# A two-layer streaming encoder on one core: last scaling on ScalarE, one transpose earlier, two orders changed where the down units open

## The reference

```python
for layer in range(DEPTH):                       # two layers: mixer A, then mixer B
    x = x + 0.5 * swiglu_ffn(rms_norm(x, ffn1_norm[layer]), ...)
    x = x + mixer(rms_norm(x, mix_norm[layer]))
    x = x + 0.5 * swiglu_ffn(rms_norm(x, ffn2_norm[layer]), ...)
return rms_norm(x, final_norm)

def swiglu_ffn(x, w_gate_up, w_down):
    g, u = split(x @ w_gate_up)
    return (silu(g) * u) @ w_down
```

## Time and profile before

| | us |
|---|---|
| three runs: median, lowest, highest | 1786.98, 1783.23, 1788.59 |
| the profiled execution: time | 1787.7 |
| its span | 1785.8 |
| PE busy | 1723.8 (97% of the span) |
| DVE busy | 1411.4 (79%) |
| ACT busy | 1009.8 (57%) |
| POOL busy | 434.9 (24%) |

### The profile page before, as it was taken

The page is one execution under the profiler, slowest core; times in us unless marked ns, Lnnn a source line. Parts: engine busy times, 40 slices in busy tenths (PEclk is TensorE's granted clock), DMA queues, the critical chain, the costliest instruction groups (busy, mean ns, idle before and its releaser), DMA issues. The chain is left out here.

```text
span 1785.8 us, 35301 instructions
## 1 busy us (share of the span) xinstructions
PE 1723.8 (97%) x12929; PEld 1612.4 (90%) x12929; DVE 1411.4 (79%) x2769; ACT 1009.8 (57%) x2008; POOL 434.9 (24%) x495
## 2 busy tenths in 40 slices
PE   8999999999999999999999999999999999999996
PEld 7999999977899999998999999987867889999995
DVE  6887887667778878867788788767897778878788
ACT  6564665446665655555665565543565556565552
POOL 2333333011023333330233333200000043333310
PEclk8999999999999999999999999999999999999998
DMA  6999899443449998994699989834112389998961
GB/s 189 203 202 212 193 200 237 100 116 90 135 104 201 199 218 196 202 220 128 132 205 201 212 200 203 195 100 120 28 41 60 124 182 200 208 214 194 209 160 48
DMA packets 170377, 293.80 MB, mean 165 GB/s; under 512 B 22689, under 2 KB 56670, under 8 KB 170206
## 3 DMA queue, kind: packets, MB, share of 16 engines
q0 software_dynamic: 66816, 121.66, 39.8%
q1 hardware_dynamic: 101824, 168.13, 31.0%
q10 hardware_dynamic: 1566, 1.74, 0.3%
HBM read 163.29 MB, written 2.10 MB: 93 GB/s over the span
## 5 line engine op out<-in xcount | busy, mean ns | idle before, releaser
L2004 PE MATMUL bank<-h_all,w_all 128*128 128x256 f32 x2352 | 671.9, 286 | 23.7 <-ACT work L1131 11.3
L2005 PE MATMUL bank<-h_all,w_all 128*128 128x256 f32 x2352 | 665.9, 283 | 0.0
L2006 PE MATMUL bank<-h_all,w_all 128*128 128x256 f32 x2352 | 665.8, 283 | 0.0
L829 POOL DMA_DIRECT2D work<-r_all x348 | 306.6, 1021 | 964.1 <-DVE w_all L1323 589.6
L2004 PEld LDWEIGHTS bank<-h_all,w_all 128*128 128x128 f32 x2352 | 451.3, 192 | 35.1 <-DVE w_all L1323 20.1
L2005 PEld LDWEIGHTS bank<-h_all,w_all 128*128 128x128 f32 x2352 | 451.6, 192 | 0.0
L2006 PEld LDWEIGHTS bank<-h_all,w_all 128*128 128x128 f32 x2352 | 451.6, 192 | 0.0
L1323 DVE TENSOR_TENSOR w_all<-work,w_all 128x512 fp32r<-128x512 f32 x352 | 234.0, 687 | 106.7 <-ACT w_all L947 106.1
L1323 DVE TENSOR_TENSOR w_all<-r_all,w_all 128x512 fp32r<-128x512 f32 (+1 forms) x356 | 300.0, 864 | 2.5 <-ACT w_all L947 0.4
L947 ACT ACTIVATE w_all<-r_all 128x512 fp32r<-128x512 f32 (+1 forms) x356 | 266.5, 768 | 58.2 <-PE bank L2006 56.8
L947 ACT ACTIVATE w_all<-work 128x512 fp32r<-128x512 f32 x352 | 209.4, 622 | 101.9 <-PE bank L2006 55.3
(11 more groups left out here) (226 smaller groups left out, 2673.3 us busy)
## 6 DMA issues: line engine op xcount, KB each, us to landing
work<-r_all POOLq DMA_DIRECT2D x348, 256.0 KB, 4.7
r_all<-ffn_gu SPq DMA_DIRECT2D x88, 512.0 KB, 5.0
r_all<-r_all POOLq DMA_DIRECT2D x116, 256.0 KB, 6.5
r_all<-ffn_gu SPq DMA_DIRECT2D x88, 256.0 KB, 6.0
work<-ffn_gu SPq DMA_DIRECT2D x88, 256.0 KB, 5.1
r_all<-ffn_d SPq DMA_DIRECT2D x32, 512.0 KB, 5.0
x_f<-ffn_e SPq DMA_DIRECT2D x24, 384.0 KB, 5.3
work<-ffn_d SPq DMA_DIRECT2D x32, 256.0 KB, 4.3
```

The costliest lines, as they stand in the source:

```text
L829: pool.dma_start(chain[g % CHAIN], plain[(u + 2) % 3][:, part * S:(part + 1) * S], accum_op=ALU.add).then_inc(chain_sum[g % CHAIN], 16)
L2004: t.matmul(o, wh, xh, start=c == 0 and not on, stop=False, skip_group_check=on)
L2005: t.matmul(o, wh, xl, start=False, stop=False, skip_group_check=on)
L2006: last = t.matmul(o, wl, xh, start=False, stop=c == PAIRED - 1, skip_group_check=on)
```

## The change

There are four edits.

1. At the end, the scaling of both halves moves from DVE to ACT (`scaled_out`). DVE makes one more small instruction a tile, the whole factor in `st[:, 5]`. ACT squares tile i and then scales tile i-1; the last tile is scaled behind all squares. DVE's order in a tile is now: both sums, the first gain, the mean, the second gain, the factor.
2. One of the twelve squares behind the units moves into unit 28, behind fill FC.
3. In units 9 and 21 (`mixed_late`) the split of the last pair moves: on ACT behind the copy `u_3`, on DVE behind the opening unit's first addition to x.
4. At the openings P6(u) stands ahead of P3(u-1), as everywhere else.

```diff
+def mixed_late(u):
+    return u in COMBINED and opening(u + 1)
...
 def product_order():
...
-        late = [(3, u - 1), (6, u)] if opening(u) else [(6, u), (3, u - 1)]
-        out += [(1, u), (2, u), (4, u - 1)] + late + [(5, u), (7, u)]
+        out += [(1, u), (2, u), (4, u - 1), (6, u), (3, u - 1), (5, u), (7, u)]
...
 # scalar block, ffn
-                    if q is not None:
+                    if q is not None and not mixed_late(u):
                         high_mixed(y_mix, combine_count(f, q, True), q % PAIRED)
                     if gate:
                         act.wait_ge(prod_done, product_count(f, 7, u))
                         act.wait_ge(e_5, at)
                         a.activation(u_3, b[:, 0:HN], ACT.Copy).then_inc(e_7, 1)
+                    if mixed_late(u):
+                        high_mixed(y_mix, combine_count(f, q, True), q % PAIRED)
...
 # scalar block, the end
+            def scaled_out(i):
+                act.wait_ge(tok_rms, i + 1)
+                act.wait_ge(tok_o, 2 * i + 2)
+                for half in range(2):
+                    o = o_stage[:, (2 * i + half) * S:(2 * i + half + 1) * S]
+                    a.activation(o, o, ACT.Copy, scale=st[:, 5, i:i + 1]).then_inc(tok_out, 1)
             for i in range(TT):
                 for half in range(2):
                     act.wait_ge(tok_x, 2 * i + half + 1)
                     a.activation(xg[:, half, :], x_final(i, half), ACT.Square, scale=D ** -0.5,
                                  accum_out=sm[:, half, 0, i:i + 1]).then_inc(tok_sq, 1)
+                if i > 0:
+                    scaled_out(i - 1)
+            scaled_out(TT - 1)
...
 # vector block, ffn
                     if opening(u):
                         dve.wait_ge(prod_done, product_count(f, 1, u))
                         x_added(UNITS[u][2], 0, b).then_inc(e_1, 1)
+                    if mixed_late(u - 1):
+                        q = COMBINED[u - 1]
+                        low_mixed(y_mix, combine_count(f, q, True), q % PAIRED)
                     low_fill(f, FU, u + 1)
...
                     low_fill(f, FC, u)
                     if q is not None:
                         mix(q % 2, k, 2)
+                    if f == FFNS - 1 and u == NU - 2:
+                        x_turned(range(4, 5))
...
-                    if q is not None:
+                    if q is not None and not mixed_late(u):
                         low_mixed(y_mix, k, q % PAIRED)
...
 # vector block, the end
-            x_turned(range(2 * (NU - 3 - DOWN_END[1]), TT * TT))
+            x_turned(range(5, TT * TT))
...
+            for i in range(TT):
+                token_sum(i, 0)
+                token_sum(i, 1)
+                token_gain(i, 0)
+                token_mean(i)
+                token_gain(i, 1)
+                token_factor(i)
...
 # in token_factor, in place of the two scalings
+                v.tensor_scalar(st[:, 5, one], st[:, 4, one], st[:, 1, one], None, ALU.mult).then_inc(tok_rms, 1)
```

More of the change, by code:

```diff
@@ L582, in build @@
         tok_out = sem("tok_out")
+        tok_o = sem("tok_o")
+        tok_rms = sem("tok_rms")
         block = ctx.enter_context(nc.Block())
@@ L1910, in _, with token_sum, token_gain, token_mean @@
             dve.wait_ge(xt_done, TT * TT)
-            for i in range(TT):
-                one = slice(i, i + 1)
[L1913 to L1921, removed]
+            def token_sum(i, half):
+                at = 2 * i + half
+                x_t = x_final(i, half)
+                dve.wait_ge(tok_full, at + 1)
+                v.scalar_tensor_tensor(x_t, TOK[at][:, :], -0.5, x_t, ALU.mult, ALU.add).then_inc(tok_x, 1)
+            def token_gain(i, half):
+                at = 2 * i + half
+                dve.wait_ge(tok_x, at + 1)
+                v.tensor_tensor(o_stage[:, at * S:(at + 1) * S], x_final(i, half), sq[:, half, :], ALU.mult
+                                ).then_inc(tok_o, 1)
+            def token_mean(i):
+                one = slice(i, i + 1)
                 dve.wait_ge(tok_sq, 2 * i + 2)
@@ L1924, in _, with token_factor @@
                                 ).then_inc(tok_mean, 1)
+            def token_factor(i):
+                one = slice(i, i + 1)
                 dve.wait_ge(pow_done, count["stat"] + i + 1)
@@ L1928, in _ @@
                 tok_done(v.tensor_scalar(st[:, 4, one], st[:, 2, one], -0.5, 1.5, ALU.mult, ALU.add))
-                for half in range(2):
-                    v.tensor_scalar(o[half], o[half], st[:, 4, one], st[:, 1, one], ALU.mult, ALU.mult
-                                    ).then_inc(tok_out, 1)
+                v.tensor_scalar(st[:, 5, one], st[:, 4, one], st[:, 1, one], None, ALU.mult).then_inc(tok_rms, 1)
[6 more added lines that the diff above has]
+                token_factor(i)
         @block.tensor
@@ L2056, in ffn @@
                     product(f, 4, u - 1)
[L2057 to L2062, removed]
+                    product(f, 6, u)
+                    product(f, 3, u - 1)
                     product(f, 5, u)
```

## The result

The changed kernel is slower: 1793.0 us median of 19 runs (1784.7 to 1797.68) against 1784.5 (1780.31 to 1788.59, 19 runs) for the kernel before. The ratio is 1.0042, interval 1.0029 to 1.0054, so 7.5 us; the two medians differ by 8.5. The forecast was 1787.9, with a range up to 1791.5: +0.9 us on 1786.98, the median of the first three runs of the kernel before, which is 2.5 above that of all 19. The profiled execution of the changed kernel took 1794.84 us with a span of 1793.0, 7.2 us more than the span before.

A forecast was written before the change was run, and what follows sets the result against it. PE was taken to bound the kernel, with time to win only at its waits and the end after it. Openings +3.7, square 0, token tiles -2.8 make +0.9 us on the 1786.98 median: 1787.9, range 1780.5 to 1791.5.

The forecast's parts named there:

- Behind P7, PE and DVE are late by the same 0.46: After each opening's wait: both engines stay 0.46 us late, so nothing beyond that delay is lost or gained.
- the price of edits 3 and 4: At the eight openings: moved splits and new product order cost +3.7 us, bounds -2.8 and +9.1.
- the slower one: At openings, FB's split starts only where it started before, losing the whole 1.14 us slot: 1793.3 us, chance 0.10.
- Edits 3 and 4, DVE's list: At each opening DVE waits for FB's high part, so its list gets 0.46 us later and P7 waits 2.0 us.
- P6 ahead of P3: At openings the new order gives nothing, since P6 had long ended when DVE came to its addition.
- Edit 2: Square moved into unit 28: DVE's 1.26 us delay is passed around, so 0; bound -1.26.
- the sign that the prediction gave for it: At the end, the squares should end as long after PE's last P3 as before.
- Edit 1: Token tiles at the end: period 5.12 to 4.09 us, power about 0.95; -2.8 us, bounds -2.5 and -4.3.
- the first: Rival at openings: FB's copy isn't late, so DVE gains 0.35 us each instead of losing 0.46; 1778.6 us, chance 0.13.
- the second: Rival at openings: the new product order itself shortens P7's wait by 1.47 us each; 1772.4 us, chance 0.04.
- The third: Rival at openings: FB's split starts no earlier than before, each losing the whole 1.14 us slot; 1793.3 us, chance 0.10.

The follow-up runs named there:

- e2_openings: Kernel before with only the moved splits and P6 ahead of P3 at the openings, the end as before: 1797.49 us, ratio 1.0069.
- d1_delay: Kernel before with one more DVE instruction (0.34 us, result unused) ahead of P6's addition at each opening: 1794.96 us, ratio 1.0057.
- e4_order: Kernel before with only P6 put ahead of P3 at the openings, splits and end as before: 1785.68 us, ratio 1.0.
- e3_splits: Kernel before with only the last pair's splits of units 9 and 21 moved on ACT and DVE: 1797.15 us, ratio 1.0078.
- e1_end: Changed kernel with the openings of before, so only the new end and the moved square: 1781.77 us, ratio 0.9981 against the kernel before.
- e7_all_add: Changed kernel with P6's addition at the openings moved up to right behind FE's split: 1776.89 us, ratio 0.9954 against the kernel before.
- e6_end_add: Kernel before with the new end, the moved square and P6's addition at openings right behind FE's split: 1777.55 us, ratio 0.9959.
- e8_sums_beside: Changed kernel with P6's addition early at openings and the next tile's sums beside POOL's power: 1776.56 us, ratio 0.9952 against the kernel before.

## Why the prediction was wrong

The step that failed is "Behind P7, PE and DVE are late by the same 0.46, so no cover is lost or gained there", and with it the price of edits 3 and 4. The delay was right and its price was not: I followed both engines at constant speed behind the wait. The runs showed that behind the longer wait TensorE ran at half clock for 3.4 us at four of the eight openings (five in e2_openings), 1.5 us lost each time. By the ratios, the openings cost 7.5 + 3.4 = 10.9 us (12.3 in e2_openings), not 3.7. The time fell outside the range because no rival held this: the slower one was about FB's fill. That its 1793.3 stands 0.3 us from the measured median is luck, as its mechanism did not occur.

The trace of before had a sign of it that the prediction did not read. Past the start-up the longest of PE's waits is one of 2.40 us in the mixer behind f = 0, and it alone goes with a stretch at half clock, where the eight waits of 1.50 us don't:

```profile
408.95 1.11 PE L2166 MATMUL bank<-ident,work 128*128 128x128 f32 x4 [2.40 <-DVE work L1779]
...
407.00:413.00 6.00, 4.05 (x43) 3.31 (x43) 3.87 (x9) 2.65 (x8) 0.94 (x1) 0.72 0.00 0
```

Over the eleven profiled executions this wait is 2.09 to 2.71 us in nine, of which eight have the stretch at half clock, and 1.29 and 1.35 us in two (d1_delay, e4_order), which have none.

Term by term:

- *Edits 3 and 4, DVE's list.* The forecast was +0.46 an opening with FB's high part as the cause; 0.45 was measured between FD and FU. That was right, and so was P7's wait of 2.0 us (1.98).
- *P6 ahead of P3.* The forecast was nothing, and e4_order measured 1.0, so by itself this was right. The order also keeps 0.5 us of the wait away from P7 when the splits move (1.81 against 2.33 in e3_splits).
- *Clock behind P7.* This was not forecast. It is four stretches in the profiled execution, some 6 us. That at the openings it follows from the longer wait is shown by d1_delay (the longer wait alone brings it), e4_order and e7_all_add (the wait in pieces or moved: none).
- *Edit 2.* The forecast was 0, and 101.00 - 100.88 = +0.12 us was measured in e1_end, so the 1.26 was only moved. That was right, but the sign that the prediction gave for it was not: the squares do end earlier against PE's last down product (from its first matmul to the first token sum it was 1762.61 - 1738.10 = 24.51 us and is 1773.11 - 1749.85 = 23.26), because the square makes that product 1.16 us late as well.
- *Edit 1.* The forecast was -2.8 with the power at about 0.95 us and a period of 4.09; measured by the rows are -3.3, a power of 0.95 and a period of 1777.06 - 1773.11 = 3.95, then (1784.89 - 1777.06) / 2 = 3.92. The mechanism was right and the gain 0.5 us too small: the mean comes 1775.20 - 1773.11 = 2.09 us behind the first sum, where I had worked out 2.27.
- *The rivals.* FB's copy was late, so the first falls. P7's wait grew, so the second falls. The third, a loss of the whole slot, does not show either: DVE lost 0.45, not 1.14.

What stays open: why some openings keep the clock and others, with the same wait, lose it. In d1_delay, e2_openings and the changed kernel it is four, five and four of eight, and not the same ones. The length of one wait does not decide it by itself: behind the 2.07 or 2.08 us ahead of P4(29) the clock stayed at 1.00 in all five executions that have this wait (the changed kernel, e1_end, e6_end_add, e7_all_add, e8_sums_beside), and so it did behind one of 2.33 us at 558.5 in e2_openings.

## What to carry to other kernels

A wait of the engine that bounds the kernel has a price beyond its length: where TensorE waits in one piece, look at the granted clock of the stretch behind it, before and after, and put that into the bounds. A list that gets longer ahead of such a wait can be paid for by taking the instruction that releases it forward (here 0.42 us of work, moved, turned a loss of 7.5 us into a gain of 8). But count only what the list behind it doesn't take back: of 1.7 us, 0.9 came back as waits one unit later.

## What the runs showed of the hardware that was not expected

- With PE busy around them, idle times of 1.50 us left the granted clock at 1.00 at all eight openings of the kernel before and of e1_end. Idle times of 1.81 to 1.84 us were followed by a stretch of 3.4 us at 1.2 GHz at four or five of eight openings, 2.33 us (e3_splits) at seven of eight. Idle times of 0.15, 0.55 and 0.71 us at one opening left it at 1.00 at all eight (e4_order). Away from the openings, 2.07 or 2.08 us ahead of P4(29) left it at 1.00 in five executions of five.
- POOL's power of one column took 0.92 to 0.95 us beside a DVE product of two SBUF operands, and 0.54 to 0.57 beside a sum with one operand in PSUM, though both move 128x512.
